# Queries of linear attention read out of PSUM before the ninth chunk's split; expert selection ahead of expert weights; token gathering interleaved with the first gate chunks

## What is computed

```python
h = rmsnorm(x, attn_norm_g)
proj = h @ w_in                       # split into gla_q, gla_k, gla_v, gla_r, gla_lr, mb_q, ...
o_gla = gla_chunked(q, k, v, g)       # gated linear attention, then norm and silu(gla_r)
o_moba, o_mem = ...                   # causal attention, attention into 256 memory tokens
x = x + concat(o_gla, o_moba, o_mem) @ w_out
# mixture of experts: 4 groups x 8 experts, the best group, in it the best two experts
lg = h @ w_rg + b_rg; g_sel = argmax(lg); p_group = softmax(lg)[g_sel]
le = h @ w_re[g_sel] + b_re; le_top, e_loc = top_k(le, 2)
gates = p_group * softmax(le_top)
x = x + sum over the two experts of gates * ((silu(h @ w_gate) * (h @ w_up)) @ w_down)
```

## Time and profile before

| | |
|---|---|
| median of 3 runs | 1364.35 us (1359.29 to 1366.28) |
| the profiled execution | 1363.38 us, its span 1361.6 us |
| mean granted TensorE clock | 0.908 of 2.4 GHz |
| TensorE busy | 1142.8 us (84%), weight loads 842.1 us |
| VectorE, ScalarE busy | 625.7 us (46%), 483.6 us (36%) |
| DMA queue of SyncE | 367.26 MB, 70.0% of 16 engines' span |
| chain of waits | 55% TensorE, 22% DMA, 15% VectorE |

### The profile page before, as it was taken

The page is one execution under the profiler, slowest core; times in us unless marked ns, Lnnn a source line. Parts: engine busy times, 40 slices in busy tenths (PEclk is TensorE's granted clock), DMA queues, the critical chain, the costliest instruction groups (busy, mean ns, idle before and its releaser), DMA issues.

```text
span 1361.6 us, 19433 instructions
## 1 busy us (share of the span) xinstructions
PE 1142.8 (84%) x7659; PEld 842.1 (62%) x7659; DVE 625.7 (46%) x1260; ACT 483.6 (36%) x786; POOL 8.9 (1%) x54
## 2 busy tenths in 40 slices
PE   6998967767476576757899889999999898999998
PEld 5774754424132342312676478999996547899986
DVE  6767451101001010001777867755447556875543
ACT  6635411000000000002554555654335455565441
POOL 1000000000000000000000000000000000000000
PEclk9999979878787887878899879999999888999999
DMA  9638379999999999999566618575556651855420
GB/s 351 212 127 305 138 289 430 429 430 430 430 429 430 430 428 430 427 423 398 193 230 251 245 40 271 186 247 183 183 183 227 250 183 63 254 180 186 187 93 31
DMA packets 121775, 368.65 MB, mean 271 GB/s; under 512 B 9890, under 2 KB 56141, under 8 KB 110926
## 3 DMA queue, kind: packets, MB, share of 16 engines
q1 hardware_dynamic: 120604, 367.26, 70.0%
q10 hardware_dynamic: 1074, 0.08, 0.1%
HBM read 366.28 MB, written 1.05 MB: 270 GB/s over the span
## 4 chain that ended last, share of the span: by engine, by line
PE 55%; DMA 22%; DVE 15%; ACT 3%; issue 3%; SPq 1%; DVEq 0%; ACTq 0%
PE ps L1934 53%; DMA more<-in_w_up_dram 9%; DMA more<-in_w_down_dram 6%; DMA more<-in_w_gate_dram 6%; DVE ring_r L33 3%; DVE st L33 3%; PE ps L1938 2%; DVE R_c L33 2%; DVE hn L33 2%; DVE X_c L33 1%; DVE R_c_r L33 1%; DMA ring<-in_ada_w_dram 1%; DVE sc L33 1%; DVE x L33 1%; SPq L712 1%
## 5 line engine op out<-in xcount | busy, mean ns | idle before, releaser
L1934 PE MATMUL ps<-ring,xg 128*32 128x512 f32 x640 | 140.2, 729 | 123.5 <-DMA more<-in_w_gate_dram 78.1
L1934 PE MATMUL ps<-hT_r,ring_r 128*128 128x256 f32 x800 | 224.2, 280 | 0.0
L1934 PEld LDWEIGHTS ps<-ring,xg 128*32 128x32 f32 x640 | 37.3, 131 | 219.2 <-issue 219.2
L1934 PE MATMUL ps<-R_c_r,W_c_r 128*128 128x256 f32 (+1 forms) x624 | 154.6, 284 | 0.0
L33 DVE TENSOR_TENSOR ring_r<-ring,W_c_r 128x1024 fp32r<-128x1024 f32 x94 | 115.2, 1225 | 81.6 <-ACT W_c_r L33 77.3
L1934 PEld LDWEIGHTS ps<-hT_r,ring_r 128*128 128x128 f32 x800 | 152.3, 190 | 0.0
L1934 PE MATMUL ps<-R_c_r,X_c_r 128*128 128x256 f32 (+1 forms) x624 | 151.1, 283 | 0.7 <-DVE R_c_r L33 0.4
L33 DVE TENSOR_TENSOR ring_r<-ring,X_c_r 128x1024 fp32r<-128x1024 f32 x88 | 107.8, 1225 | 88.3 <-ACT X_c_r L33 84.8
L1934 PE MATMUL ps<-more,xg 128*32 128x512 f32 x384 | 136.6, 736 | 0.0
L33 DVE TENSOR_TENSOR x<-x,ps 128x512 f32<-128x512 f32 x36 | 24.8, 688 | 222.5 <-PE ps L1934 222.2
L33 ACT ACTIVATE W_c_r<-ring 128x1024 fp32r<-128x1024 f32 x94 | 99.6, 1060 | 72.7 <-PE ps L1934 67.3
(11 more groups left out here) (292 smaller groups left out, 1882.6 us busy)
## 6 DMA issues: line engine op xcount, KB each, us to landing
ring<-in_ada_w_dram SPq DMA_DIRECT2D x24, 2048.0 KB, 8.6
ring<-in_w_gate_dram SPq DMA_DIRECT2D x20, 2048.0 KB, 16.8
ring<-in_w_up_dram SPq DMA_DIRECT2D x20, 2048.0 KB, 18.7
ring<-in_w_down_dram SPq DMA_DIRECT2D x20, 2048.0 KB, 17.4
more<-in_w_gate_dram SPq DMA_DIRECT2D x12, 2048.0 KB, 26.2
more<-in_w_up_dram SPq DMA_DIRECT2D x12, 2048.0 KB, 27.6
more<-in_w_down_dram SPq DMA_DIRECT2D x12, 2048.0 KB, 26.2
ring<-in_ffn_gate_dram SPq DMA_DIRECT2D x22, 1024.0 KB, 5.5
```

The source lines that it names most:

```text
L1934: return pe.matmul(out, lhsT, rhs, start=start, stop=stop, skip_group_check=True)
```

## The change

Three edits. **First place:** `then_gqk` on VectorE is cut in two; its reading of PSUM becomes `evacuate_gqk`, called before chunk 8 is fed, and the adding of later work stays where it was. **Routing:** ScalarE scales both halves of `hn`; the second mask goes to `wo`, so that `rk` is free for the ranks; `s_rank` is raised after the third of the five products, the last two go to bank 2; ranks and `sel` are made before the routing weights. **Group 0:** `gather(0)` is gone. `up(0, 0)` gathers three eighths, two, two and one ahead of its four pieces, and VectorE copies quarters (`gathered_first`). The gates' turning is cut in two with `turned_x` between, and ScalarE's copies of `x` stand between its copies of `sT`. All `s_gx` and `s_xg` counts move up by two.

```diff
@@ scalar
-            copy(hn[:, 1, :], x[:, 1, :], scale=st[:, 25:26], up=s_hn1)
+            copy(hn[:, 1, :], x[:, 1, :], scale=st[:, 25:26], up=s_hn)
+            copy(hn[:, 0, :], x[:, 0, :], scale=st[:, 24:25], up=s_hn)
...
                     for n in range(4):
+                        if n == 2:
+                            act.wait_ge(s_xt, 1)
+                            for k, b in enumerate((2, 5)):
+                                copy(xT[:, 2 * k:2 * k + 2, :], two(ps[b][:, :], 2), up=s_xta)
                         act.wait_ge(s_tg, n + 1)
...
@@ vector
-            def then_gqk():
+            def evacuate_gqk():
                 dve.wait_ge(s_rxt, 1)
                 V(dve.tensor_copy, rxS, ps[2][:, 0:256])
...
                 V(tt, lrT[0:16, :], ps[3][0:16, 0:256], rxS[0:16, :], ALU.mult, up=s_lr)
+
+            def then_gqk():
                 lanes.add(work_mem())
...
             feed(first["mqk"] + 3)
+            evacuate_gqk()
             feed.product(first["gv"], 4, lambda: None)
...
-            V(tt, rk[:, :, :], iot2, wide(ex2[:, :, 1:2], 32), ALU.is_equal)
-            V(tt, M[:, :, :], wt[:, :, :], rk[:, :, :], ALU.add, up=s_M)
-            V(ts, hn[:, 0, :], x[:, 0, :], st[:, 24:25], None, ALU.mult, up=s_hn0)
-            dve.wait_ge(s_exp, 1)
...
+            V(tt, wo[:, :, :], iot2, wide(ex2[:, :, 1:2], 32), ALU.is_equal)
+            V(tt, M[:, :, :], wt[:, :, :], wo[:, :, :], ALU.add, up=s_M)
             r_ = rk[:, :, :]
             dve.wait_ge(s_rank, 1)
...
+            def gathered_first(q):
+                dve.wait_ge(s_gx, q + 1)
+                V(tt, xg[:, 0, 2 * q:2 * q + 2, :], two(ps[6 + q % 2][:, 0:256], 2),
+                  g_ffn[:, 2 * q:2 * q + 2].unsqueeze(2).to_broadcast([128, 2, 128]), ALU.mult, up=s_xg)
...
             select(0)
+            dve.wait_ge(s_exp, 1)
+            V(dve.tensor_reduce, pg[:, :, 0], eg, AXX, ALU.add)
...
+            gathered_first(0)
+            gathered_first(1)
             V(ts, wo[:, :, :], r_, float(NS), None, ALU.is_ge)
             V(tt, wo[:, :, :], wo[:, :, :], wt[:, :, :], ALU.mult)
...
-            gathered(0)
...
+            gathered_first(2)
+            slot_weights(0)
+            gathered_first(3)
+            dve.wait_ge(s_tg, 2)
+            slot_weights(1)
@@ tensor
-            mm(ps[3][:, 32:64], strict[:, :], M[:, 1, :], False, True)
-            mm(ps[3][:, 64:96], ones[:, :], M[:, 0, :], True, False)
-            mm(ps[3][:, 64:96], ones[:, :], M[:, 1, :], False, True).then_inc(s_rank, 1)
...
+            mm(ps[3][:, 32:64], strict[:, :], M[:, 1, :], False, True).then_inc(s_rank, 1)
+            free[3] = (s_sel, 2)
+            take(2)
+            mm(ps[2][:, 64:96], ones[:, :], M[:, 0, :], True, False)
+            mm(ps[2][:, 64:96], ones[:, :], M[:, 1, :], False, True).then_inc(s_rank, 1)
...
+            def gather_first(d):
+                q = d // 2
+                if d % 2 == 0:
+                    take(6 + q % 2)
+                    pe.wait_ge(s_sel, 2)
+                for a in range(2):
+                    t = mm(ps[6 + q % 2][:, 128 * (d % 2):128 * (d % 2) + 128], hn[:, a, d::8], sel[:, 0, a], a == 0, a == 1)
+                if d % 2:
+                    t.then_inc(s_gx, 1)
+                    free[6 + q % 2] = (s_xg, q + 1)
...
                 for q in range(4):
+                    if m == 0:
+                        for k in ((0, 1, 2), (3, 4), (5, 6), (7,))[q]:
+                            gather_first(k)
+                        pe.wait_ge(s_xg, q + 1)
                     n = 12 * g + 4 * m + q
...
-            gather(0)
             for g in range(NX // 4):
                 up(g, 0)
                 if g == 0:
-                    turned_gates()
+                    turned_gates(0)
                     turned_x()
+                    turned_gates(1)
```

More of the change, by code:

```diff
@@ L363, in build @@
         s_ct, s_cols = sem("s_rows_turned"), sem("s_cols")
-        s_ss, s_rs, s_hn0, s_hn1 = [sem("s_" + n) for n in ("ss", "rstd", "hn0", "hn1")]
+        s_ss, s_rs, s_hn = [sem("s_" + n) for n in ("ss", "rstd", "hn")]
         s_rx, s_rxt = sem("s_rstd_spread"), sem("s_rstd_turned")
@@ L1054, in scalar @@
                         copy(sT[:, 4 * h:4 * h + 4, 128 * a:128 * a + 128], two4(ps[6 + n % 2][:, :]), up=s_sT)
-                    act.wait_ge(s_xt, 1)
-                    for k, b in enumerate((2, 5)):
-                        copy(xT[:, 2 * k:2 * k + 2, :], two(ps[b][:, :], 2), up=s_xta)
                     act.wait_ge(s_rowlam, 1)
@@ L1683, in overflow, with slot_weights @@
                 V(dve.tensor_copy, st[:, 90:91], st[:, 88:89])
[L1685 to L1693 removed]
+            def gathered_first(q):
+                dve.wait_ge(s_gx, q + 1)
+                V(tt, xg[:, 0, 2 * q:2 * q + 2, :], two(ps[6 + q % 2][:, 0:256], 2),
+                  g_ffn[:, 2 * q:2 * q + 2].unsqueeze(2).to_broadcast([128, 2, 128]), ALU.mult, up=s_xg)
+            def slot_weights(a):
                 bw = wt[:, a, :].unsqueeze(2).to_broadcast([128, 32, 32])
@@ L1697, in vector @@
                 V(tt, slots_w, slots_w, bw, ALU.mult, up=s_sw)
+            select(0)
+            dve.wait_ge(s_exp, 1)
+            V(dve.tensor_reduce, pg[:, :, 0], eg, AXX, ALU.add)
+            dve.wait_ge(s_exp, 2)
+            V(ts, pg[:, :, 1:2], w2[:, :, 1:2], 1.0, None, ALU.add)
+            V(dve.reciprocal, pg, pg)
+            V(dve.tensor_copy, w2[:, :, 0:1], pg[:, :, 1:2])
+            V(tt, w2[:, :, 1:2], w2[:, :, 1:2], pg[:, :, 1:2], ALU.mult)
+            V(tt, w2, w2, wide(pg[:, :, 0:1], 2), ALU.mult)
+            V(tt, wt[:, :, :], wt[:, :, :], wide(w2[:, :, 0:1], 32), ALU.mult)
+            V(tt, wo[:, :, :], wo[:, :, :], wide(w2[:, :, 1:2], 32), ALU.mult)
+            V(tt, wt[:, :, :], wt[:, :, :], wo[:, :, :], ALU.add)
+            gathered_first(0)
+            gathered_first(1)
+            V(ts, wo[:, :, :], r_, float(NS), None, ALU.is_ge)
+            V(tt, wo[:, :, :], wo[:, :, :], wt[:, :, :], ALU.mult)
+            dve.wait_ge(s_rank, 2)
+            V(dve.tensor_reduce, st[:, 88:89], ps[2][:, 64:96], AXX, ALU.max)
+            V(dve.tensor_copy, flag[0:1, 0:1], st[0:1, 88:89], up=s_flag)
+            gathered_first(2)
[3 more added lines that the diff above has]
+            slot_weights(1)
             dve.wait_ge(s_xt, 1)
@@ L2362, in gather @@
                     t.then_inc(s_gx, 1)
-                    free[6 + h] = (s_xg, 2 * g + h + 1)
+                    free[6 + h] = (s_xg, 2 * g + h + 3)
             def up(g, m):
                 take(m)
-                if m == 0:
-                    pe.wait_ge(s_xg, 2 * g + 2)
+                if m == 0 and g:
+                    pe.wait_ge(s_xg, 2 * g + 4)
                 if whole(g, ("w_gate", "w_up")[m]):
@@ L2390, in up, with turned_gates @@
                 free[m] = (s_mul if m else s_si, g + 1)
-            def turned_gates():
-                for n in range(4):
+            def turned_gates(a):
+                for n in range(2 * a, 2 * a + 2):
                     take(6 + n % 2)
@@ L2468, in overflow @@
                     pe.wait_ge(s_y, 2 * LATE)
-                    pe.wait_ge(s_xg, 2 * LATE + 2)
+                    pe.wait_ge(s_xg, 2 * LATE + 4)
                     for c in range(8):
```

25 lines of the change are left out of this document (3 added, 22 removed).

## The result

The changed kernel took 1359.18 us in the median of 18 executions (1352.32 to 1363.10), the kernel before, on the same chip and between them, 1367.8 us (18 executions, 1359.29 to 1375.58). The ratio is 0.9933, with a 95% interval of 0.9912 to 0.9955: 0.67% faster. The profiled execution took 1356.37 us, its span 1354.7 us. A ratio is given as the comparison of all executions yields it; it isn't the quotient of the two medians.

The account below looks back on a forecast made before the run. Bound: TensorE and VectorE work ahead of the ninth weight piece's issue, then the full DMA stream. -1.3 - 1.3 - 5.1 + 0.5 = -7.2 us on the profiled 1363.38 gave 1356.2 us, range 1351.8 to 1361.5.

Parts of the forecast that it names:

- First place: VectorE's reading of queries and keys moves ahead of one split: -1.3 us, bounds -0.7 and -4.7.
- Routing: Between `M` and gathering, ranks and `sel` come ahead of the routing weights: -1.3 us.
- Gathering in turn: From start of gathering to ninth issue, gathering alternates with gate pieces: -5.1 us, bounds -5.8 and -4.1.
- One cost: In group 0, the last gate piece waits 0.6 us for its copy, behind slot weights.
- the bound of 0.7 for a rise that stays where it is in time: At the first place, if the clock rises at an unchanged time, half of 1.33 us is lost: -0.7.
- the clock doesn't fall, idle time now 3.0 us: Rival at the first place: the shorter idle time keeps the clock up, 3.4 us more gain, 1352.8 us; chance 0.10.
- Stream: Weight stream after the ninth issue: thins by +0.3 us, plus +0.2 for spaced issues; bounds 0 and +1.5.
- The narrow point: The issue behind `down(0)`, at 226.2 us: stream empty at 227.9, new issue at full flow by 228.6; +0.3 us.
- no stretch under 400 GB/s: Sign to look for: the weight stream never below 400 GB/s between the ninth piece and 620 us.
- The slower rival: In group 0 the clock doesn't rise as gathering and products alternate: +15 us there, 1377 in all; chance 0.04.

Follow-up runs that it names:

- the warm-up: The changed kernel with five products that nobody reads in TensorE's wait for `M`: 1360.08 us, ratio 0.9963.
- e10_first_again: The kernel before with the first place's edit alone, run a second time: 1364.83 us, ratio 1.0000.
- filling: The changed kernel with chunk 5's product ahead of the turning on TensorE, first run as e5_fill: 1357.51 us, ratio 0.9957.
- e4_down_first: The changed kernel with group 1 gathered behind `down(0)`, not ahead of it: 1358.02 us, ratio 0.9935.
- e7_all: The changed kernel with e4_down_first, e5_fill and the warm-up together: 1357.52 us, ratio 0.9954.
- e9_best: The changed kernel with e8_fill_aligned and e4_down_first together: 1355.47 us, ratio 0.992.
- e2_whole: The changed kernel with all eight eighths of group 0 gathered ahead of gate piece 0: 1361.75 us, ratio 0.9961.
- e0_before: The kernel before, unedited, run again against itself: 1365.85 us, ratio 0.9998.
- e5_fill: The changed kernel with chunk 5's product ahead of the turning, and turning and gate product one chunk later: 1357.51 us, ratio 0.9957.
- e8_fill_aligned: e5_fill with one empty step fewer in the gate's chain on TensorE: 1357.41 us, ratio 0.9938.
- e11_after_again: The changed kernel, unedited, run again: 1360.66 us, ratio 0.9952.

## Why the prediction was right, and where it was not

The time came out at 1359.18 us against 1356.2, inside the range, and the profiled execution at 1356.37. On the ratio to runs beside it the gain is 9.2 us (0.67% of 1367.8), over all batches 6.1 (medians 1359.3 of 30 executions and 1365.4 of 129), against 7.2 predicted. Step by step:

**Routing: right.** `M` to gathering 4.53 in all four traces of the old order, 3.15 to 3.16 in all of the new without the warm-up: 1.38 against 1.3. The nine weight operations lie beside the gathering as costed, and the quarter's copy at 185.68 waits for the product (0.29 us idle), not for them.

**Gathering in turn: right, with its two outcomes.** Predicted 10.68 to 5.5 (4.9, and 0.6 for the clock). Measured 5.11 to 5.28 where the clock is back at full before piece 0 is far, 6.30 to 6.36 where it isn't: both inside the bounds. What the step missed is that the old order has two outcomes as well, 10.7 and 12.2 to 12.4. There the clock rises during gathering and falls again behind the wait for the copy, so that gate pieces run at half rate. The stretches of e10_first_again, gathering, then piece 0 and the following, then the rise again:

```profile
186.60:190.00 3.40, 2.59 (x12) 2.41 (x12) 0.74 (x2) 0.00 (x0) 0.00 (x0) 1.00 0.00 0
190.00:193.40 3.40, 3.38 (x16) 0.91 (x20) 2.40 (x2) 0.00 (x0) 0.00 (x0) 0.50 0.02 5
193.40:195.00 1.60, 1.60 (x20) 0.56 (x16) 0.00 (x0) 0.00 (x0) 0.00 (x0) 0.99 0.66 113
```

The mean of four is 11.47, that of the seven in turn without the warm-up 5.69: 5.8 us. But the two later outcomes are the two traces of the old order that have the first edit, and the two earlier ones those that don't; against the latter alone the gain is 5.0. Two traces a side can't tell an effect of that edit from chance. The Trainium skill (TensorE: Matmul & The Clock Gate, Part 1) says that the moment of the change of clock differs from run to run; the traces agree for both orders, and I had weighed it against the new order alone.

One cost had the right size and the wrong cause: the last piece waits 0.52 us for its copy (0.6 was put down), but behind its own gathering, as VectorE had been done with the slot weights for 1.02 us.

**First place: mis-sized by its clock, and the rival was put on the wrong cause.** The 1.3 us of VectorE's split came (reads at 30.64 to 31.05 instead of 31.93 to 32.19). With a fast start 0.74 us of it were left at the norm, near the bound of 0.7 for a rise that stays where it is in time. The rival "the clock doesn't fall, idle time now 3.0 us" asked whether 3.0 us makes it fall: it did, in three traces of three. What I took for fixed was the idle time. It is TensorE's arrival that varies, by 2 us, with the rate of its first products at 12 us; with a slow start the idle time is 1.0 to 1.3 and the rival's gain comes after all. Its chance was 0.10; six starts in fourteen were slow. Mean 1.6 us at the norm. The prediction carried its -1.3 unchanged from there to the end, and that step isn't borne out: from the norm to `M` the three traces without the edit take 77.7 us in the mean, the seven with it and without filling 79.2; the five of them in which the clock falls near 112 us take 78.9 to 80.5, the other two 77.7 and 77.9. With a fast start `M` is ready at 178.5 us without the edit and at 180.0 with it, with a slow one at 177.4 and 175.7. Whether the edit brings this fall, by moving all that follows, or whether three traces happened not to show it, no run settles.

**Stream: right place, too small.** The narrow point was named, the issue behind `down(0)` against an empty queue; its ninth-to-handover time was put at 39.0 (187.2 to 226.2) and measured at 39.84, so the queue was empty longer. The excess is there by the twelfth issue, 11.52 us behind the ninth instead of 3.7, 3.7 and 3.3, since a turn of two eighths and a piece takes 4.0 us. So 0.6 us were lost there instead of 0.3, and 0.3 to 0.8 for the spaced issues instead of 0.2. Ninth to ada has the mean 446.28 in the four old traces and 447.89 in the six of the changed order: 1.6 us instead of 0.5, just past the bound of 1.5. By bytes it is 1.1 to 1.5. The forecast "no stretch under 400 GB/s" was wrong: 348 for four microseconds.

**Sum.** -1.6 for the first place up to the norm, -7.1 for routing and turns together (`M` to the ninth issue: 16.0 in the four old traces, 8.9 in seven of the new), +1.6 for the stream: -7.1, where -7.2 was predicted. That it comes so close is luck. In these terms errors of about a microsecond had opposite signs, and the stretch from the norm to `M` is in neither sum. With its +1.5 the sum is -5.6, and with only the two old traces that lack the first edit (`M` to the ninth issue 15.2 us) it is -4.9; the medians over all batches say -6.1. Up to the ada wait the routing and the turns carry nearly all of the gain, and the first place, -1.6 at the norm, has about 0.1 of it left at `M`; what lies behind the ada wait spreads by more than either (last column). e4_down_first, e7_all and e9_best take back half of the stream's debt or more by bytes (0.7 and 0.4 left), but only 0.3 us of it at the ada wait.

**The slower rival** (no rise of the clock in group 0) did not come: in every trace of the new order the clock was at 1.00 by the second piece.

**Still open.** The end of the ada wait is later than the bytes say: in e2_whole the stream is 0.1 us late from 4 MB to 188 MB, and the wait ends 1.0 late (447.31 against 446.28). In the six traces of the new order the ada wait is later than the bytes by -0.1 to 1.0 us, 0.4 in the mean, so that part of their 1.6 comes from the last few pieces, behind 188 MB, and no run told what they wait for.

The kernel before has 54 of its 129 executions above 1367 us, the changed one none of 30, everything but the first edit none of 12, and the first edit alone 4 of 24. No milestone explains it: in the one trace of such an execution of the kernel before, e0_before (span 1371.9), 9.9 of the 10.3 us of excess over the first trace are in the second block, behind the ada wait (731.8 instead of 721.9 us), in unedited code. TensorE is at half clock there for 83.4 us instead of 73.5, which accounts for 5 of them. That the edits make such executions rarer is seen; why, isn't. It is also why a comparison of medians gives 6 us in one batch and 9 in another.

## What to carry to other kernels

Where TensorE waits in a dense stretch, price the wait twice: once as time, and once as what the clock takes behind it; and ask whether its *arrival* there is fixed, since an engine that comes later has a shorter wait and may lose nothing. When transfers stop because all buffers are full, order the work so that the first buffer comes free earliest, which here paid even though the same products were only put in turn; then recompute the next hand-over with the new start, because a stream that starts earlier also runs dry earlier. And price each edit between milestones in several traces, as executions that differ by 10 us elsewhere hide a gain of 1; but follow it past the next place where the clock can fall, since here 1.6 us at one milestone were 0.1 at the next.

## What was unexpected of the hardware

- TensorE's first products ran at half rate from 12 to about 16 us in six of fourteen traces (17 records instead of 32 in 3.5 us) under a granted-clock column of 1.00. The column has no event to go by there: the record of the clock begins at 15.1 to 16.4 us in these six and at 9.4 to 11.3 in the other eight. The Trainium skill (TensorE: Matmul & The Clock Gate, Part 1, Seeing it yourself) warns that the clock's trace events can't be fully trusted; here the first event agrees with the products (in e4_down_first they start 0.21 us apart up to 16.1 and 0.12 from 16.3 on, the event is at 16.2), and it is the density of records that shows the rate ahead of it.
- With the first edit in, a slower start brings the norm forward: 96.8 to 97.2 instead of 99.8 to 100.2, since the clock doesn't fall at the first place. It holds up to `M` (174.6 to 176.8 instead of 179.1 to 180.6 us, without filling).
- The same waits of at most 1.3 us at 103 to 114 us were followed by a fall of the clock in five of ten traces without filling, and not in the other five.
- The clock fell in e9_best at 35.2 us with only 0.20 and 0.58 us of idle time at the first place, and stayed up in e5_fill and e8_fill_aligned with 0.20 and 0.26. Short waits are no promise.
- Pieces of 2 MB issued 3.9 us apart, each 4.9 us long at full flow, lose 0.3 to 0.8 us against three issued at once. The first four microseconds behind the ninth issue are alike (0.98 to 1.05 MB moved in all fourteen traces); the loss comes in the next eight, across the hand-overs from piece to piece, in e11_after_again from 188.72 us on, columns as in rows 2:

```profile
188.72:192.72 4.00, 4.00 (x25) 2.44 (x26) 2.85 (x3) 0.00 (x0) 0.00 (x0) 1.00 1.01 393
192.72:196.72 4.00, 3.48 (x26) 1.85 (x27) 0.45 (x2) 0.00 (x0) 0.00 (x0) 1.00 0.98 397
```

In the kernel before, at the same distance from its ninth issue (197.63 to 201.63 and 201.63 to 205.63), it is 430 and 426 GB/s; in the first trace of the changed kernel (192.69 to 196.69 and 196.69 to 200.69) it is 414 and 418.
